# Stick-breaking attention: fp32 sums replaced by two rounded products, one for the high and one for the low part

## What is computed

```
z = einsum("bhqd,bhkd->bhqk", qb, kb) * scale
log_not = where(mask, log_sigmoid(-z), 0.0)
later = cumsum(log_not, axis=3, reverse=True) - log_not
wts = where(mask, exp(log_sigmoid(z) + later), 0.0)
out = einsum("bhqk,bhkd->bhqd", wts, vb)
```

## Time and profile before

| | us |
|---|---|
| median of 3 runs | 947.11 |
| lowest and highest | 946.62 to 947.29 |
| the profiled execution's own time | 946.43 |
| span of its profile | 944.70 |
| first scores to output projection, in the span | 331.95 to 356.39 |

### The profile page before, as it was taken

One profiled execution on the slowest core, in us unless ns is written; L12 is line 12 of the kernel. 1 busy time (PEld: TensorE's weight loads), 2 busy tenths in 40 slices (PEclk: granted clock), 3 DMA queues, 4 the chain that ended last, 5 costly groups with the idle time before them and its releaser, 6 DMA issues.

```text
span 944.7 us, 13417 instructions
## 1 busy us (share of the span) xinstructions
PE 936.2 (99%) x5240; PEld 790.5 (84%) x5240; DVE 636.3 (67%) x878; ACT 508.5 (54%) x677; POOL 42.6 (5%) x109
## 2 busy tenths in 40 slices
PE   9999999999999999999999999999999999999997
PEld 8878888888888987888888888877777888888886
DVE  6895777775456465777777348598884676775444
ACT  6664655554345664755555336657685455544333
POOL 2600000000000000000000001000400000000000
PEclk9999999999999999999999999999999999999999
DMA  9535554555555320655555549543234555555551
GB/s 357 182 112 192 186 180 178 189 205 184 185 181 210 138 89 24 213 197 191 178 190 206 204 178 335 203 139 130 94 121 143 179 179 185 202 191 200 197 204 44
DMA packets 25579, 167.62 MB, mean 177 GB/s; under 512 B 2733, under 2 KB 3611, under 8 KB 6459
## 3 DMA queue, kind: packets, MB, share of 16 engines
q1 hardware_dynamic: 24176, 162.34, 48.8%
q0 software_dynamic: 1264, 4.57, 1.3%
q10 hardware_dynamic: 91, 0.04, 0.0%
HBM read 165.86 MB, written 1.08 MB: 177 GB/s over the span
## 4 chain that ended last, share of the span: by engine, by line
PE 96%; DVE 3%; ACT 1%; issue 0%; DVEq 0%
PE ps L1676 44%; PE ps L1995 23%; PE ps L2003 12%; PE ps L2100 2%; PE ps L1831 2%; PE ps L1793 1%; PE ps L2432 1%; PE ps L2442 1%; PE ps L2461 1%; PE ps L2142 1%; DVE w_both L997 1%; PE ps L1752 1%; PE ps L1906 1%; PE ps L1809 1%; PE ps L1954 0%
## 5 line engine op out<-in xcount | busy, mean ns | idle before, releaser
L997 DVE TENSOR_TENSOR w_both<-raw,w_both 128x2048 fp32r<-128x2048 f32 x149 | 340.5, 2292 | 141.7 <-ACT w_both L525 141.6
L525 ACT ACTIVATE w_both<-raw 128x2048 fp32r<-128x2048 f32 x149 | 283.4, 1910 | 132.3 <-DMA raw<-in_down 40.8
L1995 PE MATMUL ps<-a_both,w_both 128*128 128x512 f32 x960 | 230.7, 391 | 0.0
L1995 PEld LDWEIGHTS ps<-a_both,w_both 128*128 128x128 f32 x960 | 176.2, 188 | 33.6
L1676 PE MATMUL ps<-w_both,a_both 128*128 128x512 f32 (+1 forms) x768 | 178.9, 388 | 0.0
L1676 PEld LDWEIGHTS ps<-w_both,a_both 128*128 128x128 f32 x768 | 138.2, 188 | 29.0 <-issue 2.6
L1676 PE MATMUL ps<-w_both,h_hi 128*128 128x512 f32 x576 | 154.6, 390 | 0.0
L2003 PEld LDWEIGHTS ps<-a_both,w_both 128*128 128x128 f32 x960 | 123.9, 191 | 5.2
L1676 PEld LDWEIGHTS ps<-w_both,h_hi 128*128 128x128 f32 x576 | 107.8, 188 | 22.0
L2003 PE MATMUL ps<-a_both,w_both 128*128 128x256 f32 x960 | 125.5, 283 | 0.0
L1676 PE MATMUL ps<-w_both,h_lo 128*128 128x512 f32 x288 | 88.8, 390 | 0.0
(11 more groups left out here) (288 smaller groups left out, 841.2 us busy)
## 6 DMA issues: line engine op xcount, KB each, us to landing
raw<-in_a_gu SPq DMA_DIRECT2D x22, 1024.0 KB, 4.7
raw<-in_b_gu SPq DMA_DIRECT2D x22, 1024.0 KB, 4.7
raw<-in_up SPq DMA_DIRECT2D x16, 1024.0 KB, 4.8
raw<-in_down SPq DMA_DIRECT2D x16, 1024.0 KB, 4.8
raw<-in_a_down SPq DMA_DIRECT2D x11, 1024.0 KB, 4.8
raw<-in_b_down SPq DMA_DIRECT2D x11, 1024.0 KB, 4.7
raw<-in_front SPq DMA_DIRECT2D x8, 1024.0 KB, 4.8
raw<-in_gates SPq DMA_DIRECT2D x8, 1024.0 KB, 4.8
```

The lines of the kernel that those rows point to most:

```text
L525: A_(ring(w_hi, us)[:, 0:n], ring(raw, us)[:, 0:n], ACT.Copy).then_inc(s_hi, 1)
L997: V.tensor_tensor(ring(w_lo, us)[:, 0:n], ring(raw, us)[:, 0:n], ring(w_hi, us)[:, 0:n].bitcast(fp32), ALU.subtract).then_inc(s_lo, 1)
L1995: ins = MM(bank(4 * k + s).rearrange("p (z n) -> p z n", z=2), ring(w_hi, us)[:, at:at + P], both_parts[:, :, c, :], start=c == 0, stop=False)
```

## The change

The sums are no longer fp32 products. POOL rounds the softplus of each head to fp32r (`sb_hi_r`, in the place of `sbE`), and the rest, softplus minus high part, goes to `sb_lo_r` in the place of `sbL` itself: for the first head on VectorE (the new `sb_rest`, below **rest**), for the second on POOL, behind its two casts. TensorE multiplies the triangle and the ones, which ScalarE rounds once into `sb_sum_r`, with the high parts (`sb_sums_hi`) and with the low parts (`sb_sums_lo`), and the scores of pair p + 2 stand between the two. The triangle is now applied to all 384 columns in one product. ScalarE takes exp and ln of pair 1 ahead of the loop and then of p + 2 behind the weights of p. VectorE takes pair p + 2 through neg, plus and rest in a row. Since high parts lie where `sbE` was, neg of pair p + 2 now waits for the sums of pair p.

```diff
@@ -171,10 +171,13 @@
         kTB = over("kTB", 6 * S)
         mkTB = over("mkTB", 512)
         sbE = over("sbE", 2 * 2 * 384)
+        sb_hi_r = place("sb_hi_r", 2 * 2 * 384, f32r, at=cur["at"] - 2 * 2 * 384)
         sbL = over("sbL", 2 * 2 * 384)
+        sb_lo_r = place("sb_lo_r", 2 * 2 * 384, f32r, at=cur["at"] - 2 * 2 * 384)
         sbW = over("sbW", 2 * 2 * 384)
         sb_neg_r = place("sb_neg_r", 2 * P, f32r, at=cur["at"])
-        cur["at"] += 2 * P
+        sb_sum_r = place("sb_sum_r", 2 * P, f32r, at=cur["at"] + 2 * P)
+        cur["at"] += 4 * P
         memPB = over("memPB", 4 * 512)

         cur["at"] = r1
@@ -211,6 +214,7 @@
         s_z, s_abs, s_sbe, s_sbl, s_tri, s_wt, s_sbpv = (sem(n) for n in ("sb_scores", "sb_negated", "sb_log1p",
             "sb_softplus", "sb_summed", "sb_weights", "sb_mixed"))
         s_neg, s_ptd = sem("sb_mask_rounded"), sem("probsT_copied_dve")
+        s_sbh, s_sbq0, s_sbq1 = sem("sb_softplus_hi"), sem("sb_softplus_lo_first"), sem("sb_softplus_lo_second")
         s_rTq, s_rbq = sem("query_rms_turned"), sem("query_rms_rows")
         s_sg, s_hb, s_ht, s_hhi, s_hlo = (sem(n) for n in ("gate_act", "hidden", "hidden_transposed",
                                                          "hidden_hi", "hidden_lo"))
@@ -277,7 +281,7 @@
         def ring(t, u):
             return t[:, (u % NRAW) * UNIT:(u % NRAW + 1) * UNIT]

-        sb_tri, sb_ones = sbc[:, 0:P], sbc[:, P:2 * P]
+        sb_tri, sb_ones = sb_sum_r[:, 0:P], sb_sum_r[:, P:2 * P]
         sb_neg = sbc[:, 512:1024].rearrange("p (z n) -> p z n", z=2)[:, :, P:2 * P]


@@ -462,6 +466,14 @@
             pool.wait_ge(s_tab, 1 + len(BUCKETS))
             pool.dma_start(A["table"], stage[0:16, 0:512]).then_inc(s_tabd, 16)

+            for p in range(6):
+                for e in range(2):
+                    pool.wait_ge(s_sbl, 2 * p + e + 1)
+                    nc.gpsimd.tensor_copy(sb_half(sb_hi_r, p, e), sb_half(sbL, p, e)).then_inc(s_sbh, 1)
+                pool.wait_ge(s_sbh, 2 * p + 2)
+                nc.gpsimd.tensor_tensor(sb_half(sb_lo_r, p, 1), sb_half(sbL, p, 1), sb_half(sb_hi_r, p, 1).bitcast(fp32),
+                                        ALU.subtract).then_inc(s_sbq1, 1)
+
             pool.wait_ge(s_mm, U0["b_down"] + 1)
             pool.wait_ge(s_hlo, 22)
             pool.dma_start(gfin[:, :], A["final_norm"].partition_broadcast(P)).then_inc(s_gfin, 16)
@@ -763,6 +775,7 @@
             act.preload_act_table_set("natural_log_exp_and_others")
             act.wait_ge(s_sbc, 16)
             A_(sb_neg_r[:, :].rearrange("p (z n) -> p z n", z=2), sb_neg, ACT.Copy).then_inc(s_neg, 1)
+            A_(sb_sum_r[:, :], sbc[:, 0:2 * P], ACT.Copy).then_inc(s_neg, 1)

             def sb_softplus(p):

@@ -796,9 +809,11 @@
             def sb_hi(p):
                 pair_hi((O0["sb"] + p, p), s_sbpv, p + 1)
             sb_softplus(0)
+            sb_softplus(1)
             for p in range(5):
-                sb_softplus(p + 1)
                 sb_weights(p)
+                if p < 4:
+                    sb_softplus(p + 2)
                 if p:
                     sb_hi(p - 1)
             mem_exps("mem_b", 0)
@@ -1302,7 +1317,7 @@
                     dve.wait_ge(s_z, 2 * p + e + 1)
                     z = bank(SB_BANK[p % 3] + e, 0, 384)
                     if p >= 2:
-                        dve.wait_ge(s_sbl, 2 * p - 3 + e)
+                        dve.wait_ge(s_tri, 2 * p - 3 + e)
                     V.tensor_scalar(sb_half(sbE, p, e).bitcast(i32), z.bitcast(i32), -2 ** 31, None, ALU.bitwise_or)                        .then_inc(s_abs, 1)

             def sb_plus(p, heads=(0, 1)):
@@ -1313,6 +1328,12 @@
                         dve.wait_ge(s_tri, 2 * p - 3 + e)
                     V.scalar_tensor_tensor(sb_half(sbL, p, e), bank(SB_BANK[p % 3] + e, 0, 384), 0.0,
                                            sb_half(sbE, p, e), ALU.max, ALU.add).then_inc(s_sbl, 1)
+
+            def sb_rest(p):
+
+                dve.wait_ge(s_sbh, 2 * p + 1)
+                V.tensor_tensor(sb_half(sb_lo_r, p, 0), sb_half(sbL, p, 0), sb_half(sb_hi_r, p, 0).bitcast(fp32),
+                                ALU.subtract).then_inc(s_sbq0, 1)

             def sb_lo(p):
                 pair_lo((O0["sb"] + p, p))
@@ -1321,17 +1342,20 @@
             sb_negated(1, (0,))
             sb_plus(0, (1,))
             sb_negated(1, (1,))
+            sb_rest(0)
             dve.wait_ge(s_mm, U0["q"] + 4)
             queries(1)
-            for p in range(5):
-                sb_plus(p + 1)
-                if p + 2 < 6:
-                    sb_negated(p + 2)
-                else:
-                    mem_max("mem_b", 0)
-                    mem_max("mem_b", 1)
+            sb_plus(1)
+            sb_rest(1)
+            for p in range(4):
+                sb_negated(p + 2)
+                sb_plus(p + 2)
+                sb_rest(p + 2)
                 if p:
                     sb_lo(p - 1)
+            sb_lo(3)
+            mem_max("mem_b", 0)
+            mem_max("mem_b", 1)
             mem_norm("mem_b", 0)
             mem_norm("mem_b", 1)
             sb_lo(4)
@@ -2134,16 +2158,23 @@
                     MM(bank(banks[e], 256, 384), kTB[r, c + P:c + S], qTB[r, c + P:c + S], start=False, stop=False,
                        skip_group_check=True).then_inc(s_z, 1)

-            def sb_sums(p):
-
+            def sb_sums_hi(p):
+
+                pe.wait_ge(s_neg, 2)
                 for e in range(2):
                     b = SB_BANK[p % 3] + e
-                    pe.wait_ge(s_sbl, 2 * p + e + 1)
-                    MM(bank(b, 0, 256), sb_tri, sb_half(sbL, p, e, 0, 256), start=False, stop=False,
+                    pe.wait_ge(s_sbh, 2 * p + e + 1)
+                    MM(bank(b, 0, 384), sb_tri, sb_half(sb_hi_r, p, e), start=False, stop=False, skip_group_check=True)
+                    MM(bank(b, 128, 256), sb_ones, sb_half(sb_hi_r, p, e, 256, 384), start=False, stop=False,
                        skip_group_check=True)
-                    MM(bank(b, 128, 256), sb_ones, sb_half(sbL, p, e, 256, 384), start=False, stop=False,
-                       skip_group_check=True)
-                    MM(bank(b, 256, 384), sb_tri, sb_half(sbL, p, e, 256, 384), start=False, stop=True,
+
+            def sb_sums_lo(p):
+
+                for e in range(2):
+                    b = SB_BANK[p % 3] + e
+                    pe.wait_ge((s_sbq0, s_sbq1)[e], p + 1)
+                    MM(bank(b, 0, 384), sb_tri, sb_half(sb_lo_r, p, e), start=False, stop=False, skip_group_check=True)
+                    MM(bank(b, 128, 256), sb_ones, sb_half(sb_lo_r, p, e, 256, 384), start=False, stop=True,
                        skip_group_check=True).then_inc(s_tri, 1)

             def sb_values(p):
@@ -2208,16 +2239,18 @@
                 pe.wait_ge(s_olo, O0["sb"] + c + 1)
                 out_columns(c // 2, 0, (c % 2,))
             for p in range(5):
-                sb_sums(p)
+                sb_sums_hi(p)
                 if p == 1:
                     pe.wait_ge(s_gdve, emptied(G0["q"] + 1, "dve"))
                 if p + 2 < 6:
                     sb_scores(p + 2)
+                sb_sums_lo(p)
                 if p:
                     sb_values(p - 1)
             pe.wait_ge(s_wt, 4)
             mem_logits("mem_b", 0, qTB[:, 6 * S:8 * S], mkTB)
-            sb_sums(5)
+            sb_sums_hi(5)
+            sb_sums_lo(5)
             out_piece(0)
             sb_values(4)
             out_piece(1)
```

## The result

The changed kernel takes **949.37 us** (median of 9 runs, 948.73 to 950.77) and the kernel before 947.11 (9 runs, 946.62 to 947.52): a ratio of 1.0027, with a 95% interval of 1.0019 to 1.0036. It is slower by 2.3 us. The profiled execution took 950.1 us, 0.7 over its median. In ten profiles of this study the stage begins anywhere from 331.95 to 332.93, also where nothing ahead of it was edited, so stages are compared by their length and not by where they end.

The account below looks back on a forecast made before the run. TensorE was taken to bound the kernel; its 3.9 us saving turns into waits as VectorE's queue sets the pace: start 1.55 late, steps 3.94 + 4.28 + 4.28, then the tail, +2.4 us, 949.5 us, range 947.9 to 952.0.

Parts of the forecast that it names:

- The chain in VectorE's queue: In the loop, VectorE's neg, plus and rest in a row take 3.94 or 4.28 us, above TensorE's 3.85.
- the second rival: POOL's casts take 0.79 us each, like its first, five times over: +5.2 us, 952.3; chance 0.12.
- The port: VectorE's rest and POOL block each other: rest ends 0.41 us after the second cast, POOL's subtraction 0.87 after rest.
- the first rival: Rest gets in before POOL's cast, or neither blocks the other: +1.1 to +1.6 us, 948.2 to 948.7; chance 0.22.
- The start: Ahead of the loop, VectorE's neg of pair 2 begins at 340.99 instead of 339.44, 1.55 us late.
- The tail: After neg of pair 5 (353.49): casts, rest, POOL's subtraction and TensorE's last products, ending at 358.81.
- TensorE's saving: A pair's sums on TensorE cost 1.13 us instead of 1.78: 3.9 us saved for six, period 3.2.
- Busy time of the page: TensorE's busy time over the whole kernel falls by some 4 us while the span grows.
- The order before: In the kernel before, VectorE's order lets ScalarE's exp and ln of one pair run while VectorE does another.
- TensorE gets slower: Narrow fp32r at four times the price, or a lower granted clock during waits: some +10 us, 957; chance 0.06.
- The look-ahead: It hides VectorE's chain and TensorE keeps the pace: 3.9 us off but about 1 in the tail, 944.2; chance 0.05.

Follow-up runs that it names:

- rest later: The changed kernel with rest of pair p + 1 moved on VectorE between neg and plus of pair p + 2: 946.12 us.
- The best kernel here: The changed kernel with rest moved between neg and plus of the next pair, and pair 0 keeping its fp32 sums: 945.60 us.
- order alone: The kernel before, fp32 sums kept, with only the new order of VectorE and ScalarE: 947.00 us, ratio 1.0002.
- more in the queue: The changed kernel with one more VectorE instruction, an unread maximum over 384 columns, behind each rest: 952.04 us.

## Why the prediction was right

The forecast was 949.5 and +2.4 us, and 949.37 and +2.3 came out, within its narrow range (948.7 to 950.5). By its steps:

- **The chain in VectorE's queue.** Steps of 3.94 and 4.28 were forecast, 3.93 and 4.27 measured. Neg to plus: 2.01 and 2.01. The casts took 0.50, also the very first, so that the second rival (0.79) had nothing for it (its sum is also 0.1 too high: five times 0.54 is 2.7).
- **The port.** Rest was to end 0.41 behind the second cast, and does (0.41), and POOL's subtraction 0.87 behind rest (0.86). Five of six rests take 0.84, and the first rival wanted 0.55. The Trainium skill (SBUF — State Buffer, Who interferes with whom) says that whichever of the two is issued first has the port for its whole instruction and the other is blocked meanwhile; the trace agrees in both directions, with POOL ahead (0.84, and 1.24 with rest later) and with VectorE ahead (1.19 on POOL, where 1.01 is the price alone).
- **The start.** Neg of pair 2 was forecast 9.04 after the scores (340.99 - 331.95) and came 8.98 and 8.99 after them.
- **The tail.** From neg of pair 5 to the output projection: 358.81 - 353.49 = 5.32 forecast, 5.26 measured with the clock at 1.00. The wait of 0.05 was as estimated, and the weight load put at 0.10 cost 0.05 (the first product 0.28 and not 0.23). In the first profile TensorE at the lower clock ended the stage instead, 0.48 later.
- **TensorE's saving, mis-sized.** A pair of sums was to cost 1.13 us in place of 1.78, with a period of 3.2. In a turn where nothing waits the period is 3.40, a saving of 0.45 a pair and not 0.65. The two products of a head come to the forecast sum, though neither price was right (0.23 + 0.06 where 0.17 + 0.11 stood), but the first of each group costs 0.05 more and the step to the values 0.09 more, twice and once a pair: 0.63 for the high and 0.72 for the low group. It did not touch the sum, since TensorE was no longer the bound, but it takes a third off what can be had: 2.7 us for six pairs and not 3.9. The best kernel here gained 1.3.
- **Busy time of the page.** It was to fall by some 4 us; it rose from 936.2 to 936.7 in one profile and fell to 935.5 in the second. The stage's own fell by 1.6 (24.40 to 22.77) where the prediction took 3.9: the saving was smaller (above, 0.45 x 6 = 2.7), and a product ahead of a wait counts to its modelled end (0.22 for 128 columns that otherwise make way after 0.06), up to 0.16 at each of nine waits. That is enough for the 1.1 that are left, but was not measured apart. What lies outside the stage differs by 0.9 from one profile to another (936.2 - 24.40 = 911.8 against 935.5 - 22.77 = 912.7).
- **The order before, told wrongly.** The prediction said that in the kernel before VectorE's order lets exp and ln of one pair run while VectorE works on the other. Its cyclic order was neg, m_lo, plus all along, with the wait of about 1.00 for ScalarE, as the earlier trace rows show, and the order alone costs nothing. What is new in the queue is rest with its round trip through POOL, about 1.0, and an m_lo that no longer fills the wait for ScalarE (0.34). The numbers were worked out from the new order and did not hang on that sentence.
- **The rivals.** TensorE gets slower: its second half came true in part. The clock fell for about 3 us in one of two profiles, and that cost 0.5 and not 10: the rival had it lower over four periods, and it fell only at the end of the stage, where part of TensorE's loss went into waits that it had anyway. The look-ahead hides nothing as built; with rest in another place it does, and TensorE keeps the pace, at its true price.

## What to carry over

A bound engine that hands work to an idle one gains only if the engines between them have room: here VectorE had about 0.5 to 1 us in a period of 3.85, and one instruction that waits for another engine in the middle of its queue took more than that. Where such an instruction stands in the queue decides: put it where the queue waits for something else already (rest between neg and plus), and the same work is nearly free. For the first turn of a loop, which has no neighbour to hide its latency, the older, longer form on the bound engine can be the faster one: here it took 0.5 us off the stage. The last turn, which has none either, was not tried.

## What the runs showed of the hardware

- Where VectorE's subtraction of two SBUF tiles and a cast or subtraction on POOL overlap, the one that began later pays what is left of the other's time, and then its own less about 0.14 us: 0.56 became 0.84 behind a cast and 1.24 behind a subtraction, and POOL's 1.01 became 1.19. A cast of the same size on ScalarE (0.52) beside VectorE's subtraction cost it nothing (0.56).
- In a run of fp32r products on TensorE, each with a weight load of its own (0.19 us) beside it, the next product starts 0.23 us after one of 384 columns and 0.06 after one of 128.
- The granted clock fell to 0.50 in the stage in two profiles of ten (the changed kernel's first and that with more in the queue), each time behind a stretch of waits of up to 0.7 and 1.2 us, and not in the changed kernel's second profile, with the same waits.
